# Four modulation vectors: from TensorE matmuls with a column of c to VectorE sums over half buffers

## The reference, cut to what matters

```python
c_act = jax.nn.silu(c)                                  # 1 x 2048
mod = c_act @ w_ada[l] + b_ada[l]                       # 2048 x 12288
shift1, scale1, gate1, shift2, scale2, gate2 = jnp.split(mod, 6, axis=-1)
h = modulate(rms_norm(x, norm_mix_g[l]), shift1, scale1)
...
merged = sigmoid(g_sb) * (y_sb @ p_sb[l]) + sigmoid(g_s5) * (y_s5 @ p_s5[l]) + sigmoid(g_ml) * (y_ml @ p_ml[l])
x = x + gate1[:, None, :] * (merged @ w_out[l])
h = modulate(rms_norm(x, norm_moe_g[l]), shift2, scale2)
x = x + gate2[:, None, :] * hierarchical_moe(h, ...)
```

## Time and profile before

| | us |
|---|---|
| three runs | 3178.5, 3186.3, 3190.9 |
| median | 3186.3 |
| profiled execution, first to last instruction | 3191.1 |
| TensorE matmuls busy | 2895.9 (91%) |
| VectorE, ScalarE, GpSimd busy | 1298.4 (41%), 1189.4 (37%), 1677.8 (53%) |

### The profile page before, as it was taken

One profiled execution on the slowest core, in us unless ns is written; L12 is line 12 of the kernel. 1 busy time (PEld: TensorE's weight loads), 2 busy tenths in 40 slices (PEclk: granted clock), 3 DMA queues, 4 the chain that ended last, 5 costly groups with the idle time before them and its releaser, 6 DMA issues.

```text
span 3191.1 us, 51532 instructions
## 1 busy us (share of the span) xinstructions
PE 2895.9 (91%) x19920; PEld 2395.3 (75%) x19920; DVE 1298.4 (41%) x2025; ACT 1189.4 (37%) x1458; POOL 1677.8 (53%) x1274
## 2 busy tenths in 40 slices
PE   6999979999999999858798878889999999999998
PEld 1688777887998878733343338789988989998998
DVE  1488833224453242331222224347723253325344
ACT  1233343333454332320110104556744446654343
POOL 0000067687786776400000004967779997779797
PEclk8899989999999999978998988989999999999999
DMA  9533337467343586649999972533445554445443
GB/s 390 204 125 115 125 132 298 177 238 289 149 150 139 206 295 252 226 170 394 422 381 401 415 308 89 190 138 140 150 145 187 188 182 158 158 149 192 160 167 127
DMA packets 98628, 679.76 MB, mean 213 GB/s; under 512 B 11584, under 2 KB 15424, under 8 KB 16832
## 3 DMA queue, kind: packets, MB, share of 16 engines
q1 hardware_dynamic: 83088, 602.97, 50.1%
q10 hardware_dynamic: 15408, 74.85, 6.2%
HBM read 770.05 MB, written 2.10 MB: 242 GB/s over the span
## 4 chain that ended last, share of the span: by engine, by line
PE 56%; DMA 9%; DVE 3%; ACT 3%; POOL 2%; issue 1%; SPq 1%; ACTq 0%; DVEq 0%; POOLq 0%
PE acc L567 36%; PE wk L567 7%; PE acc L640 7%; DMA ring<-in_moe 7%; PE acc L644 4%; PE acc L653 2%; DMA side_buf<-in_ada 2%; POOL w_lo L549 2%; ACT w_hi L1296 1%; SPq L499 1%; ACT hb L1296 0%; DVE hb L1857 0%; ACT L1296 0%; DMA stage<-in_main 0%; DVE dl L1857 0%
## 5 line engine op out<-in xcount | busy, mean ns | idle before, releaser
L549 POOL TENSOR_TENSOR w_lo<-stage,w_hi 128x512 fp32r<-128x512 f32 x1268 | 1670.6, 1351 | 1465.1 <-ACT w_hi L1296 969.0
L1296 ACT ACTIVATE w_hi<-stage 128x2048 fp32r<-128x2048 f32 x317 | 603.7, 1906 | 42.4 <-DMA stage<-in_main 42.0
L567 PE MATMUL acc<-xhl,w_hi 128*128 128x256 f32 x4064 | 526.1, 288 | 27.6 <-DVE xhl L1857 10.2
L567 PEld LDWEIGHTS acc<-xhl,w_hi 128*128 128x128 f32 x4064 | 509.5, 196 | 31.6 <-ACT w_hi L1296 12.0
L640 PE MATMUL acc<-xhl,w_hi 128*128 128x512 f32 x1536 | 371.2, 394 | 0.0
L640 PEld LDWEIGHTS acc<-xhl,w_hi 128*128 128x128 f32 x1536 | 281.6, 188 | 92.6 <-issue 37.7
L567 PE MATMUL acc<-xhl,w_lo 128*128 128x256 f32 x2032 | 271.7, 287 | 0.0
L567 PEld LDWEIGHTS acc<-xhl,w_lo 128*128 128x128 f32 x2032 | 256.7, 194 | 3.0 <-issue 2.5
L567 PE MATMUL acc<-h,stage 128*128 128x256 f32 x1024 | 235.8, 386 | 2.9 <-ACT h L1296 2.9
L567 PEld LDWEIGHTS acc<-h,stage 128*128 128x128 f32 x1024 | 193.6, 192 | 40.6 <-issue 15.1
L644 PEld LDWEIGHTS acc<-xhl,w_lo 128*128 128x128 f32 x1536 | 196.9, 191 | 7.5
(11 more groups left out here) (486 smaller groups left out, 4042.0 us busy)
## 6 DMA issues: line engine op xcount, KB each, us to landing
stage<-in_main SPq DMA_DIRECT2D x317, 1024.0 KB, 4.8
ring<-in_moe SPq DMA_DIRECT2D x192, 1024.0 KB, 10.4
side_buf<-in_ada ACTq DMA_DIRECT2D x64, 1024.0 KB, 4.9
over_lo<-in_moe ACTq DMA_DIRECT2D x48, 1024.0 KB
over_hi<-in_moe ACTq DMA_DIRECT2D x42, 1024.0 KB
stage<-in_ada SPq DMA_DIRECT2D x32, 1024.0 KB, 8.6
stage<-in_sb SPq DMA_DIRECT2D x32, 1024.0 KB, 4.8
x<-in_x ACTq DMA_DIRECT2D x1, 2048.0 KB, 12.9
```

The lines of the kernel that those rows point to most:

```text
L549: last = pool.tensor_tensor(w_lo[:, k % 2, cs], stage[:, k, cs], w_hi[:, k, cs].bitcast(F32), ALU.subtract)
L567: return pe.matmul(o, w, r, start=start, stop=stop)
L1296: return act.activation(o, i, f, **kw)
```

## The change

The products of `w_ada` with c move from TensorE to VectorE. `side_buf` is the same 8 KB per partition, but it is two halves of 1024 columns, each with its own load (512 KB) and its own semaphore (`side_in[0]`, `side_in[1]`). For each tile t VectorE takes half b, multiplies every partition by its element of c and adds it to a running sum in two banks of `wk` (b = 0: banks 0 and 1, b = 1: banks 2 and 3), so the sum is 128 x 2048. ScalarE's `side_next` waits for one half and issues its next load, then for the other half. At the end ScalarE copies all four banks to `side_row` (128 x 2048, over the same bytes as the buffer), and TensorE adds over the 128 partitions: 16 matmuls with a block of `side_row` as weights and one column of ones (`side_columns`) in place of 16 x 4 + 4.

```diff
-    side_buf = [sb(f"side_buf{u}", [P, CH], at=at) for u, at in enumerate(side_at)]
-    side_row = [sb(f"side_row{u}", [P, 512], at=at) for u, at in enumerate(side_at)]
+    side_buf = [sb(f"side_buf{u}", [P, 2, CH // 2], at=at) for u, at in enumerate(side_at)]
+    side_row = [sb(f"side_row{u}", [P, CH], at=at) for u, at in enumerate(side_at)]
...
-        def side(u, t):
-            pe.wait_ge(side_in, 16 * (u * 16 + t) + 16)
-            ada_part(side_buf[u], t, 2 + u % 2).then_inc(side_used, 1)
+        def side_columns(u):
+
+            v = 2 + u
+            pe.wait_ge(row_ready, v + 1)
+            for b in range(16):
+                last = mm(wk[:, 1, v * 16 + b:v * 16 + b + 1], side_row[u][:, b * P:(b + 1) * P], ones[:, 0:1])
+            last.then_inc(ada_sum, 1)
...
-        beside_ada("g_sb", 0, both)
+        each(pe, BASE["g_sb"], 16, both)
...
             deep(*slot(BASE["wout"] + t))
             if t == 1:
-                ada_columns(4, side_row[2])
-            side(3, t)
-        ada_columns(5, side_row[3])
+                side_columns(2)
+        side_columns(3)
...
         def side_next(u, t):
-            act.wait_ge(side_used, u * 16 + t + 1)
-            if t < 15:
-                side_load(u, t + 1)
-            else:
-                fn(side_row[u][:], wk[:, 2 + u % 2, :], ACT.Copy).then_inc(row_ready, 1)
+            for b in range(2):
+                act.wait_ge(side_used, u * 32 + 2 * t + b + 1)
+                if t < 15:
+                    side_load(u, t + 1, b)
+            if t == 15:
+                fn(side_row[u][:], wk[:, :, :].rearrange("p a b -> p (a b)"), ACT.Copy).then_inc(row_ready, 1)
...
+        def side_part(u, t):
+
+            for b in range(2):
+                o = wk[:, 2 * b:2 * b + 2, :].rearrange("p a b -> p (a b)")
+                dve.wait_ge(side_in[b], 16 * (u * 16 + t) + 16)
+                c = cact[:, t:t + 1]
+                if t:
+                    dve.wait_ge(side_used, u * 32 + 2 * t + b - 1)
+                    stt(o, side_buf[u][:, b, :], c, o, MUL, ADD).then_inc(side_used, 1)
+                else:
+                    ts(o, side_buf[u][:, b, :], c, MUL).then_inc(side_used, 1)
...
                 tt(sg[:, k % 2, :], sg[:, k % 2, :], acc[:, k, T:2 * T], ADD).then_inc(sg_sum, 1)
+                if u is not None:
+                    side_part(u, t)
                 dve.wait_ge(evac_done, q * 4 + k + 1)
...
-        each(dve, BASE["wout"], 16, add_out)
+        for t in range(16):
+            add_out(*slot(BASE["wout"] + t), t)
+            side_part(3, t)
```

More of the change, by code:

```diff
@@ L287, in build @@
     ada_used = nc.alloc_semaphore("ada_used")
-    side_in = nc.alloc_semaphore("side_in")
+    side_in = [nc.alloc_semaphore(f"side_in{b}") for b in range(2)]
     side_used = nc.alloc_semaphore("side_used")
@@ L736, in _ @@
         ada_columns(1, ada_row[:, 1, :])
[L738 to L742, removed]
         def stage_a(g, s):
@@ L818, in _ @@
         each(pe, BASE["glu"], 4, half)
-        ada_columns(2, side_row[0])
+        side_columns(0)
         spin(24, BASE["p_s5"])
@@ L822, in _ @@
         each(pe, BASE["p_s5"], 8, half)
-        beside_ada("g_s5", 1, both)
+        each(pe, BASE["g_s5"], 16, both)
         each(pe, BASE["mlif"], 1, wide)
-        ada_columns(3, side_row[1])
+        side_columns(1)
         def columns():
@@ L882, in _ @@
         each(pe, BASE["p_ml"] + 4, 4, half)
-        beside_ada("g_ml", 2, both)
+        each(pe, BASE["g_ml"], 16, both)
         spin(36, BASE["wout"])
@@ L1337, in _, with side_load, side_first @@
         last.then_inc(rms_sq, 1)
-        def side_load(u, t):
-            act.dma_start(side_buf[u][:], dr["ada"][NADA + u * 16 + t]).then_inc(side_in, 16)
-        def side_next(u, t):
-            act.wait_ge(side_used, u * 16 + t + 1)
-            if t < 15:
-                side_load(u, t + 1)
-            else:
-                fn(side_row[u][:], wk[:, 2 + u % 2, :], ACT.Copy).then_inc(row_ready, 1)
+        def side_load(u, t, b):
+            act.dma_start(side_buf[u][:, b, :], dr["ada"][NADA + u * 16 + t][:, b * (CH // 2):(b + 1) * (CH // 2)]).then_inc(side_in[b], 16)
+        def side_first(u):
+            for b in range(2):
+                side_load(u, 0, b)
+        def side_next(u, t):
+            for b in range(2):
[4 more added lines that the diff above has]
+                fn(side_row[u][:], wk[:, :, :].rearrange("p a b -> p (a b)"), ACT.Copy).then_inc(row_ready, 1)
         def rms_root(c):
@@ L1466, in _ @@
         act.wait_ge(y5_ready, 9)
-        side_load(0, 0)
+        side_first(0)
         merge_p("p_sb", ptmp1)
@@ L1483, in _ @@
         act.wait_ge(ada_sum, 3)
-        side_load(1, 0)
+        side_first(1)
         merge_g("g_s5", A["sg"], u=1)
@@ L1539, in _ @@
         act.wait_ge(by_ready, 4)
-        side_load(2, 0)
+        side_first(2)
         merge_p("p_ml", ptmp1)
         merge_g("g_ml", B["sg"], u=2)
-        side_load(3, 0)
+        side_first(3)
         def wout_step(k, q, t, more=True):
@@ L2085, in _, with merge_g @@
         sg_n = [0, 0]
-        def merge_g(g, sg, pt, first=False):
+        def side_part(u, t):
+            for b in range(2):
+                o = wk[:, 2 * b:2 * b + 2, :].rearrange("p a b -> p (a b)")
[6 more added lines that the diff above has]
+                    ts(o, side_buf[u][:, b, :], c, MUL).then_inc(side_used, 1)
+        def merge_g(g, sg, pt, first=False, u=None):
             n0, m0 = sg_n
@@ L2103, in go @@
                     tt(merged[:, t, :], merged[:, t, :], sg[:, k % 2, :], ADD).then_inc(sg_used, 1)
-            each(dve, BASE[g], 16, go)
+            if u is None:
+                each(dve, BASE[g], 16, go)
+            else:
+                for t in range(16):
+                    go(*slot(BASE[g] + t), t)
             if not first:
                 sg_n[0] += 16
-        merge_g("g_sb", A["sg"], ptmp1, True)
+        merge_g("g_sb", A["sg"], ptmp1, True, u=0)
         dve.wait_ge(gelu_done, 2)
@@ L2118, in _ @@
         modulation(2)
-        merge_g("g_s5", A["sg"], ptmp1)
+        merge_g("g_s5", A["sg"], ptmp1, u=1)
         modulation(3)
@@ L2204, in _ @@
         stage_b(None, 3)
-        merge_g("g_ml", B["sg"], ptmp1)
+        merge_g("g_ml", B["sg"], ptmp1, u=2)
         def split_merged(n):
```

## The result

The changed kernel takes 3224.3 us, median of 4 runs (3222.2 to 3232.3), against 3186.6 us before on the same chip (4 runs, 3178.5 to 3190.9): a ratio of the means of 1.0126, 95% interval 1.0111 to 1.0141. It is 38 us slower, where 52 us less were forecast. The range, 3110 to 3166, doesn't hold it.

What follows compares the result with a forecast made beforehand. TensorE was taken to set the pace, with some waits on the single buffer. 83 us saved, less 10.7, 8, 8 and 4, gave 52: 3139 against the profiled span, forecast 3134 us, range 3110 to 3166.

Steps and rivals of the forecast that it cites:

- the one on loads: Loads of side_buf: a 512 KB half lands in 3.7 us, upper bound 4.9, so its round of 5.1 hides under TensorE's 5.57.
- if a half load costs as much as a whole: Loads of side_buf: one of two stated signs that the forecast is wrong; a whole 1 MB load landed in 4.9 us.
- the half loads are the bound: Rival on side_buf loads: half lands in 4.9 us, round 6.3, only 19 us gained, 3167 us; chance 0.09.
- TensorE's tile of 5.57: Three gate stages: a TensorE tile without side takes 5.57 us, against 7.06 each before.
- The sum at 1.28 us: VectorE's added scalar_tensor_tensor of 1024 columns, buffer in SBUF and sum in PSUM: 1.28 us each, 2.6 for both per tile.
- the rival at 3.39 a sum: Rival on VectorE's sums: they share the port with GpSimd and take 3.39 us each, total 3362 us; chance 0.07.
- a mix, 6.1: VectorE's tile in g_s5 and g_ml: 6.1 us, between 5.6 and 6.9, so 8 us behind in each stage.
- the rival in step: Rival in g_s5 and g_ml: VectorE's multiplication beats GpSimd's third piece, 5.6 us a tile, no lag, 3118 us; chance 0.20.
- first sum done 14 us after the first tile: Start of wout: VectorE's fourth-vector sums begin late, 14 us in place of 4.3; 4 us left at the end.
- The end of wout: Sum of squares starts 2.7 us later, and side_columns(3) with the spin ends 0.7 behind it: 3.4 us lost.
- The columns, 3.6: TensorE's adding over partitions at stage ends: 32 instructions take 3.6 us, 2.7 more than the 8 before.
- three banks ahead absorb that: ScalarE's evictions: if VectorE is late by more than 2 us, they are late too, but TensorE's banks ahead absorb it.

## Why the prediction was wrong

**The step that failed** is the one on loads: "Per tile 2 MB are loaded as before, in 5.6 us for 7.1 ... A half's round is landing 3.7, sum 1.3, issue 0.1: 5.1, under 5.57." The 3.7 isn't wrong as such. It is exactly what the last half of g_sb takes, when no other half is on its way any more:

```profile
L1337 ACTq DMA_DIRECT2D side_buf<-in_ada x1: 334/334/334, 588.0 to 588.0; - x1
...
DMA to landing us min/median/max: 3.7/3.7/3.7
```

But it is the price of a load that has the engines to itself (no other load is issued or under way in those 3.7 us), interpolated from loads of the kernel before, where one load of 1 MB for the stage and one for `side` shared the time. Measured, the median is 5.4 (up to 12.1), above the 4.9 that the prediction had as the upper bound, and on the chain of g_sb, where each late one counts, the mean is 6.0. With the sum of 1.3 that is the turn of 7.3 to 7.7, over TensorE's 5.57 and over the 7.06 of the tile before. The prediction's own sign of being wrong, "if a half load costs as much as a whole", came true.

The sentence ahead of the quoted one held a warning and wasn't worked out: the DMA engines had 0.80 of their time in use at 7.06 us a tile, so at 5.57 they need 0.80 x 7.06 / 5.57 = 1.01. With two buffers one reads 0.99 to 1.00. The changed kernel never got there (0.87), so that sum warns of longer landings but doesn't give them. That fewer bytes on their way shorten them enough is shown in two of the gates only, by the run with half the bytes; why a half takes 5.5 at a share of 0.87, where the wholes of one buffer keep their 4.9, stays open in part.

The rival "the half loads are the bound" had this mechanism, and a chance of 0.09. Its price was too low as well: its landing, 4.9, also came from the trace of the kernel before. With the measured rounds it would have been 15 x (7.33 - 5.57) = 26 in each gate stage and 15 x (7.7 - 5.76) = 29 in wout: about 108 us of lag, where it counted 11.7 in each gate and 18.5 in wout, 54 in all. Two buffers against one are worth 104.

**The other steps**, as the kernel with two buffers shows them, where loads don't interfere:

- TensorE's tile of 5.57: right, in both kernels.
- The sum at 1.28 us: right, 1288 ns (1281 with two buffers), and 1278 for the multiplication that begins a vector. No extra cost of writing PSUM shows over the estimate of 1.28, and the rival at 3.39 a sum is refuted.
- VectorE's tile in g_s5 and g_ml, "a mix, 6.1": wrong, in the good direction. From one multiplication with `ptmp` to the next are 5.56 us, 687.62 and 693.18 in the timeline above, which is TensorE's pace. That is the price of the rival in step, 5.6, with no lag: 16 us better than the forecast. It is not quite its picture: the multiplication takes 1.01 and not 0.4 to 0.6. GpSimd's pieces are 1.31 each from 684.55 on. The multiplication is issued 0.86 before the end of the third (688.48) and ends 0.15 behind it; the addition is issued during the fourth, which ends at 689.79, and ends at 690.07, 0.28 behind it. The margin was larger than the forecast's few tenths, since the two sums start 1.19 apart and the multiplication comes 3.2 after the copy, not 3.6. The Trainium skill (page SBUF — State Buffer, section SBUF: two separate sides) has the two engines exclude each other for a whole instruction; these ends, each just behind a piece, and the steady 5.56 agree with it. The mean of two phases that I took described none.
- The stages: by the forecast's terms, with VectorE in step, the start of glu, the first rows of mlif, the start of wout and `rms_red` each come earlier by another 20.5 (15 x 1.49 - 1.9), 19.7 (less 0.9 and 1.8), 19.7 (less 2.7) and 8.8 (19.8 - 3.6 - 3.4 - 4). Measured with two buffers: 22.0, 17.5, 23.9 and 7.5, together 70.9 against 68.7. The sum holds; single stages are off by up to 4, and within wout two terms that are wrong, by 4 and by 6 us, work against each other (next two points). That the sum is so close is in part luck.
- The start of wout, "first sum done 14 us after the first tile": 20.6 with two buffers, and 20.8 in the changed kernel, from the start of wout. The changed kernel's TensorE begins the columns only at 13.0 (1233.70); their 3.6, the modulation, an addition of 1.5 to `x` and the two multiplications of 2.5 come behind. With two buffers none of it is left at the end of wout, where the forecast had 4 us.
- The end of wout, where `side_columns(3)` and the `spin` were to end 0.7 behind the sum of squares: 6.7 behind with two buffers, 6.2 in the changed kernel.
- The columns, 3.6: measured 3.63 to 4.07 where TensorE was busy before. After the waits for a row they take 6.99, as in the row at 1359.88: the granted clock there is 0.50, the lower level of 1.2 GHz, and 1.00 (2.4 GHz) where they take 3.63. So each such wait costs some 3.4 us more than its length.
- What a late VectorE does: "three banks ahead absorb that". They absorb most of it for TensorE until the stage ends (within the stages it waits 3 to 9 us), and then the rest comes at once: 28.2, 17.3, 18.5 and 29.5 us.

Put together: 52 forecast, 16 more for VectorE in step, is 68; the kernel with two buffers gained 67. The kernel with one buffer is 104 us slower than that one, which makes the 38 that were lost; the 104 is a measured difference, against the 108 of the sum above. One term turned the gain into a loss: the landing of a half, which was taken for a constant. The 16, the 4 and the 0.7 were wrong too, and smaller.

## What to carry to other kernels

When a change makes the pace faster, scale the busy share of the DMA engines by it before pricing any load. If old share x old tile / new tile comes near 1, a landing time from the old trace is a lower bound and not a price: here, at shares of 0.97 to 0.98, loads of 1 MB took 4.9 us in one stage and up to 8.5 in others. With a single buffer, landing, use and issue stand in a row in every tile, and it is the mean landing that counts, not the median. Give such a stream its second buffer first (here it costs 1 MB and is worth 104 us, more than all the rest), and only then split loads. Between two engines that exclude each other, look for the phase in which they can settle rather than take the mean of two. And look again at matmuls that fill a wait when a change moves that wait.

## What the runs showed of the hardware

- The 16 DMA engines moved 376 to 380 GB/s into SBUF at a busy share of 0.99 to 1.00 with rows of 4 and 8 KB in the gates, and 415 GB/s at 1.00 in the kernel before from 1500 to 1580 us, where the experts' weights are loaded. So a share near 1 is not yet one rate. The Trainium skill (page DMA: Bandwidth & Descriptors, section Specifications) names about 358 GB/s for one core, half of the 716 of a stack; this one core was over it in all these stretches.
- Under load the size of one transfer says little of when it lands: medians of 5.5 us for 512 KB in g_sb of the changed kernel, 6.0 for 256 KB with quarters, 4.9 for 1 MB with one buffer.
- A `scalar_tensor_tensor` with one tensor in SBUF, one in PSUM, the output in PSUM and a scalar per partition takes 1288 ns for 1024 columns and 750 for 512 in float32, with GpSimd busy beside it; `tensor_scalar` from SBUF to PSUM takes no less (1278).
